# Five unrolled loops of the expert stage become hardware loops

## The reference, cut to what matters

```
idx = jnp.take_along_axis(cand_i, best_j, axis=-1)
gate = jax.nn.softmax(best_s, axis=-1)
act = jax.nn.gelu(jnp.einsum('thkd,td->thk', u_table[idx].astype(f32), xc.astype(f32)), approximate=False)
return jnp.einsum('thk,thkd->td', gate * act, v_table[idx].astype(f32)).astype(xc.dtype)
```

## Time and profile before

| | |
|---|---|
| median of 3 runs | 3418.4 us (3418.02 to 3423.0) |
| the profiled execution | 3418.02 us |
| its span | 3416.2 us |
| busy: PE, DVE, POOL, ACT | 2317.9, 2248.2, 1343.9, 1028.7 us |
| DMA moved | 1216.96 MB, 356 GB/s over the span |
| granted TensorE clock, mean | 0.826 |

### The profile page before, as it was taken

The page is one execution under the profiler, slowest core; times in us unless marked ns, Lnnn a source line. Parts: engine busy times, 40 slices in busy tenths (PEclk is TensorE's granted clock), DMA queues, the critical chain, the costliest instruction groups (busy, mean ns, idle before and its releaser), DMA issues.

```text
span 3416.2 us, 32073 instructions
## 1 busy us (share of the span) xinstructions
PE 2317.9 (68%) x9269; PEld 942.4 (28%) x9269; DVE 2248.2 (66%) x5256; ACT 1028.7 (30%) x3405; POOL 1343.9 (39%) x1241
## 2 busy tenths in 40 slices
PE   7997566575676567666765686568556856685576
PEld 4554443141133113211321142114112411151121
DVE  4433527879657955785578557856785677668754
ACT  2221213432332233223323332333233323333222
POOL 1131103334444444444444444444444444444532
PEclk9998788797788689868986888688768977897799
DMA  4222157999999999999999999999999999999998
GB/s 180 83 71 76 28 211 311 371 376 394 390 412 416 388 409 421 413 377 413 417 416 381 416 416 420 376 410 417 416 384 420 421 413 388 417 415 415 388 419 346
DMA packets 190072, 1216.96 MB, mean 356 GB/s; under 512 B 27112, under 2 KB 32664, under 8 KB 49176
## 3 DMA queue, kind: packets, MB, share of 16 engines
q0 software_dynamic: 157152, 1141.51, 82.4%
q1 hardware_dynamic: 30432, 71.87, 5.9%
q10 hardware_dynamic: 2312, 1.54, 0.2%
HBM read 1199.16 MB, written 15.55 MB: 356 GB/s over the span
## 4 chain that ended last, share of the span: by engine, by line
DMA 29%; DVE 24%; PE 21%; issue 6%; ACT 5%; POOL 2%; DVEq 0%; POOLq 0%; SPq 0%; PEldq 0%; ACTq 0%
DMA uv_ring<-in_uv_table,idx 28%; DVE uv_ring L1767 12%; PE ACC L1940 12%; PE TQ L1879 5%; POOL uv_ring L1419 2%; DVE S L1686 2%; DVE idx_f L1687 2%; DVE S L1685 2%; ACT dg L1541 2%; PE OP L1860 2%; PE TQ L1901 1%; ACT dot L1534 1%; ACT dot L1521 1%; PE ACC L1930 0%; DVE pos L1617 0%
## 5 line engine op out<-in xcount | busy, mean ns | idle before, releaser
L1940 PE MATMUL ACC<-uv_ring,dg 128*64 128x512 f32 x4352 | 1460.5, 782 | 957.0 <-ACT dg L1541 956.7
L1419 POOL DMA_INDIRECT uv_ring<-in_uv_table,idx x1088 | 1265.1, 1163 | 1707.6 <-PE ACC L1940 1402.8
L1767 DVE CUSTOM_DVE_ANT_0 uv_ring<-uv_ring,xn 128x1024 f32<-128x1024 f32 x1088 | 1322.6, 1226 | 712.8 <-DMA uv_ring<-in_uv_table,idx 668.9
L1940 PEld LDWEIGHTS ACC<-uv_ring,dg 128*64 128x64 f32 x4352 | 340.0, 165 | 1961.4 <-ACT dg L1541 1442.5
L1521 ACT ACTIVATE dot<-dot 128x2 f32<-128x2 f32 x544 | 110.6, 203 | 1798.5 <-DVE dot L1767 1798.2
L1541 ACT ACTIVATE dg<-stack,dot 128x64 f32<-128x64 f32 x1088 | 327.1, 340 | 17.8
L1534 ACT ACTIVATE dot<-gate,dot 128x1 f32<-128x1 f32 x1088 | 261.3, 287 | 18.9
L1879 PEld LDWEIGHTS TQ<-glu_and_queries,wq 128*128 128x128 f32 x2048 | 236.5, 193 | 62.8 <-issue 62.8
L1879 PE MATMUL TQ<-glu_and_queries,wq 128*128 128x128 f32 x2048 | 250.1, 280 | 0.0
L515 PE MATMUL PJ<-w_in,xT 128*128 128x512 f32 (+1 forms) x384 | 142.9, 532 | 3.2 <-DVE xT L401 3.2
L515 PEld LDWEIGHTS PJ<-w_in,xT 128*128 128x128 f32 x384 | 73.3, 193 | 72.3 <-issue 65.3
(11 more groups left out here) (338 smaller groups left out, 1696.3 us busy)
## 6 DMA issues: line engine op xcount, KB each, us to landing
uv_ring<-in_uv_table,idx POOLq DMA_INDIRECT x1088, 10.5
glu_and_queries<-in_w_glu SPq DMA_DIRECT2D x9, 1024.0 KB, 17.1
wq<-in_w_query SPq DMA_DIRECT2D x8, 1024.0 KB, 19.8
w_in<-in_w_in SPq DMA_DIRECT2D x8, 640.0 KB, 9.1
xt<-in_x SPq DMA_DIRECT2D x9, 512.0 KB, 4.6
xr<-scratch_x SPq DMA_DIRECT2D x9, 512.0 KB, 7.9
xc<-in_x_columns SPq DMA_DIRECT2D x8, 512.0 KB, 3.7
xk<-in_x SPq DMA_DIRECT2D x8, 512.0 KB, 3.4
```

The costliest lines, as they stand in the source:

```text
L1419: pool.indirect_dma_start(out=ring[:, s_ % RING, :], out_offset=None, in_=a["uv_table"], in_offset=bass.IndirectOffsetOnAxis(ap=idx[:, s_: ...
L1767: V.tensor_tensor_reduce(row, row, xn[:, g, :], 1.0, 0.0, ALU.mult, ALU.add, dot[:, s_:s_ + 1]).then_inc(dots, 1)
L1940: ins = nc.tensor.matmul(ACC[GT * g:GT * (g + 1), b, :], dg[:, n % DG, :], ring[:, n % RING, D + 512 * b:D + 512 * b + 512], start=False, ...
```

## The change

The loop over turns 1 to 6 on POOL, ACT, DVE and PE, and the loop over turns 0 to 6 on SP, become hardware loops (`Fori`): the body stands once in the program, a register holds t, and a compare-and-branch at its end jumps back. In the body every wait whose value depends on t takes it from a register, and so do SP's DRAM addresses. Turn 0, turn 7 and the samples stay written out.

DVE's own step count can no longer be a Python number, so `Steps` is replaced by `PerTile` there, which assumes 130 steps in a turn and adds t x 130 to a base.

```
+class PerTile:
+    def __init__(self, sem, per):
+        self.sem, self.n, self.base, self.per = sem, 0, 0, per
+    def chain(self, eng, t, ins, nop=False):
+        self.n += 1
+        ins.then_inc(self.sem, 1)
+        eng.wait_ge(self.sem, self.n if t is None else self.base + t * self.per + self.n)
+        if nop:
+            eng.nop(nofuse=True)
+    def loop_begins(self, t):
+        self.base, self.n = self.n - t * self.per, 0
+    def turn_ends(self):
+        assert self.n == self.per, (self.n, self.per)
+        self.n = 0
...
+        DVE_STEPS = 130
...
-        dch = c.steps("dve_steps_e")
+        dch = PerTile(c.sem("dve_steps_e"), DVE_STEPS)
...
-                for t in range(PT - 1):
+                with sp.Fori(0, PT - 1) as t:
...
-                for t in range(1, PT - 1):
+                with pool.Fori(1, PT - 1) as t:
...
-                for t in range(1, PT - 1):
+                with act.Fori(1, PT - 1) as t:
...
                 def dch_(ins, nop=False):
-                    dch.chain(dve, ins)
-                    if nop:
-                        dve.nop(nofuse=True)
+                    dch.chain(dve, turn_now[0], ins, nop)
...
-                for t in range(1, PT - 1):
+                dch.loop_begins(1)
+                with dve.Fori(1, PT - 1) as t:
                     retrieve("steady", t)
+                dch.turn_ends()
                 retrieve("eighth", PT - 1)
+                dch.turn_ends()
...
-                for t in range(1, PT - 1):
+                with pe.Fori(1, PT - 1) as t:
```

More of the change, by code:

```diff
@@ L1604, in _ @@
                 V = nc.vector
+                turn_now = [None]
                 def dch_(ins, nop=False):
-                    dch.chain(dve, ins)
-                    if nop:
-                        dve.nop(nofuse=True)
+                    dch.chain(dve, turn_now[0], ins, nop)
                 def best16(vals, where, src):
@@ L1787, in retrieve @@
                 def retrieve(turn, t):
+                    turn_now[0] = None if turn == "first" else t
                     for s_ in range(LEAD, slots_of(turn)):
```

## The result

| | median | range, runs |
|---|---|---|
| before, on the same chip | 3420.16 us | 3418.02 to 3423.0, 4 |
| after | 3442.47 us | 3440.05 to 3445.3, 4 |

A forecast was written before the change was run, and what follows sets the result against it. The kernel was taken as DMA-bound except in the matching stage, where DVE binds. 3418.0 + 0 (jumps) + 1.2 (ACT registers) + 0.3 (fetching) = 3419.5 us, no change; range 3414 to 3433 us.

The forecast's parts named there:

- What bounds the kernel: Over a turn of 337.3 us: DMA-bound, except 60 us of matching stage where DVE binds and a short dip between turns.
- The slack: Gather time from issue to landing above 5.3 us can be lost free: 5.8 us for DVE's slot 10, 4.1 for PE's slot 8.
- X: Stall of one engine at one jump back to the loop's head: taken as 3.9 us, with 0 and 8.8 kept.
- The stall of a jump: At each loop's end, the wait for program code: 3.9 us, from a small load of the same size, bounds 0 and 8.8.
- ACT, POOL, SP: nothing: At the turn's end, jumps on these three engines cost nothing; POOL's is hidden up to a stall of 7.8 us.
- The late slots of DVE are caught up: After a late slot behind the jump, DVE catches up, being busy only two thirds of the DMA-bound stretch.
- The sum with 8.8 us: At five turn ends, with the longest stall: PE 2.5 us too late, or 4.3 with DVE in full; 12 to 22 us.
- Rival 1: At turn ends the jumps lie bare, from a 6.3 us stall (PE) or 7.0 (DVE): 3426 to 3441 us; chance 0.22.
- The registers: Register operations at 0.1 us each: 1.2 us in all on ACT, in and behind the matching stage; nothing on DVE, POOL, PE.
- rival 2: In the matching stage, register operations bind DVE: 14 us slower at 0.1 us bared, 3434 us; chance 0.09.
- more to fetch, 0.3 us: Program fetching in each turn: about 510 more instructions, some 0.2 MB in all, entered in the sum as 0.3 us.
- What would show it: At ends of turns 1 to 5: DVE idle 2 to 4 us, slot 10's gather landing in some 8 us, DMA share unchanged.

The follow-up runs named there:

- e5: Kernel before, with 2000 satisfied waits more on SP, written out, in each of turns 0 to 6: 3457.8 us against 3425.94.
- e12: Kernel before, with 1000 satisfied waits more on SP, written out, in each of turns 0 to 6: 3442.82 us against 3420.99.
- e6: Kernel before, with four unused DVE operations behind norm_out of turns 1 to 5, next product 5.0 us late, no jump: 3439.64 us against 3425.94.
- e10: Kernel before, with two unused DVE operations behind norm_out of turns 1 to 5, next product 2.5 us late: 3426.79 us against 3420.99.
- e3: Changed kernel with the hardware loop on DVE only, the other engines' turns written out: 3438.86 us against 3421.92 before the change.
- e1: Changed kernel with its registers (SP has constants) but no jump back, each turn in a loop of one pass: 3429.63 us against 3421.92 before the change.
- e4: Changed kernel with the hardware loop on PE only, the other engines' turns written out: 3424.77 us against 3421.92 before the change.
- e8: Kernel before, with a hardware loop on PE only, with the prefetch hint for its jump: 3422.7 us against 3425.94.
- e9: Changed kernel with DVE alone written out again, all other loops kept: 3425.42 us against 3420.99 before the change.
- e7: Changed kernel with two turns in a body on POOL, ACT, DVE and PE, two jumps instead of five: 3438.05 us against 3425.94 before the change.

## Why the prediction was wrong

Its own steps, in its order:

- **What bounds the kernel.** Held. It is DMA-bound but for the matching stage: e5 and e12 lose time only outside it. (The DMA digits are 9 from the eighth slice on, not from the seventh, which reads 7; nothing hangs on it.)
- **The slack: the step that failed.** The prediction took what lies above 5.3 us between issue and landing as time that could be given away, and so 5.8 us for DVE and 4.1 for PE. 5.3 us is the least over all gathers, and it comes from a place where the DMA engines were not full: the gather was issued at 591 us, in turn 0. The window around it, the landings of gathers from 560 to 600 us, and those of the DMA-bound stretch of turn 1 (1250 to 1480 us), all of before:

```profile
586.00:596.00 10.00, 6.26 (x22) 1.81 (x24) 9.02 (x29) 4.88 (x14) 3.94 (x4) 0.81 0.55 211
```

```profile
DMA to landing us min/median/max: 5.3/7.7/10.2
```

```profile
DMA to landing us min/median/max: 7.3/11.4/17.3
```

  So a better bound, 7.3 us, stood in the trace of before. With it slot 8 has 2.1 us of slack and slot 10 3.8: for X = 3.9 still enough (1.7 and 2.7 late), for the stalls that came not (1.3 to 2.5 and 5.0 late). At the turn's end, with the gathers issued so late that few were on their way, a gather still needed 7.7 us at the least (gathers issued from 1250 to 1266 in the changed kernel; before, from 1243 to 1262, 9.4, 11.1 and 12.3):

```profile
DMA to landing us min/median/max: 7.7/8.2/10.1
```

  With 7.7 in place of 5.3 the slack of slot 8 is 9.4 - 7.7 = 1.7 us and of slot 10 3.4. e6 and e10 measured 2.3 and 1.3. A second fault is in the idea itself: a gather that lands 5.3 or 7.7 us after its issue did not wait, but the DMA engines are full only while several are on their way. Slots 8 and 9 are all that was issued between 1247 and 1261, and the rate was 291 to 329 GB/s against 381 to 428.
- **The stall of a jump.** X was taken as 3.9 us, with 0 and 8.8 as ends; it is 5.6 to 6.3 us on DVE (`norm_out` start to product), 4.7 to 7.1 us on ACT from the root to the table load, and by the prediction's rule X - 2.2 = 1.3 to 2.5 us some 3.5 to 4.7 us on PE. Inside the bounds, 2 us too small on DVE. This error alone would not have changed the answer: 6.3 us is below the 7.0 from which DVE's was to show. On the stall itself the trace agrees with the rule of the Trainium skill, "Runtime: NRT & Kernel Launch", section "Instruction fetch mechanics", that a taken branch to a target out of the window stops the engine until the block has come: DVE stood for 4.96 us with no data missing, and in e3 a packet of program starts inside the stall, where before has none.
- **ACT, POOL, SP: nothing.** Held. ACT's GELU behind its stall still waits 2.59 us for DVE, POOL's gathers wait for PE.
- **The late slots of DVE are caught up.** It did catch up, 2.3 us by slot 8. But that does not bring back what was not transferred: in e6 slot 3 of the next turn is still 2.6 us late.
- **The sum with 8.8 us**, 2.5 to 4.3 us at each of five jumps, 12 to 22 in all, holds the measured 15. That is luck: in this sum X was too large by some 3 us and DVE's slack by some 4, and the two errors came near to cancelling. Rival 1 named the right mechanism and the right place, PE and DVE too late for the gathers of slots 8 to 11, with a threshold that was too high by 4 us. Had the landings of before been read at this place (9.4 us at the least), slot 8 would have had no slack and slot 10 11.1 - 9.4 = 1.7 us. With X = 3.9 that makes 1.7 to 2.7 us a jump, by my estimate 8 to 14 us in all, and rival 1 the forecast.
- **The registers.** ACT's first diagonal stands 0.83 us behind the GELU instead of 0.75: +0.08, as forecast 0.1. In the matching stage nothing, so rival 2 is out. But the term "more to fetch, 0.3 us" is wrong by its kind: it divided bytes by the rate of all 16 engines. In e5 and e12 fetching cost 0.3 to 0.5 us a packet while the DMA engines were the limit, and registers with what they bring cost 7.7 us.
- **What would show it.** The gather into slot 10's place landed in 8.2 us (issued at 1261.38, taken at 1269.56), as foreseen, and I had taken that as the sign of a hidden stall. It was the sign of the opposite: a queue that is short. The DMA share fell from 1.01 to 0.91 to 0.99 behind each jump, which the prediction named as what would prove it wrong. Turn 1 took 341.3 us instead of 337.3.

The forecast failed by these two terms, the slack that it took from the wrong place and the fetching that it put at 0.3 us. The sum as the runs have it: DVE's lateness 13.7 (e6) and registers with fetching 7.7 (e1), 21.4 of 22.3 us.

## What to carry to other kernels

Slack in a DMA-bound stretch is not the longest wait minus the shortest landing of the whole run. Read the landings and the GB/s at the place in question, and ask how many transfers are on their way when the late one is issued; what DVE caught up later here did not bring back the transfers that did not run (where only PE was late, e4, a part came back). A hardware loop costs its jump where the engine that jumps closes the ring, so use the hint (here it took away 15 of 22 us), and count instruction packets as transfers: in a kernel that is DMA-bound, fewer of them were worth a little here (4 us for 33), many more were dear (31 us for 110).

## What was unexpected of the hardware

- A jump back over a body of a few hundred instructions stops DVE for 4.4 to 5.1 us beyond what lies under the operation before it, with one engine jumping (e3) as with five; with the hint, for nothing that can be seen.
- An 8 KB packet of program cost 0.34 us (e12) to 0.46 us (e5) of the whole when the DMA engines were full, and nothing in the matching stage. It was less for PE's packets (e8) and in e9.
- PE's loop with the hint is not fetched again (40 packets instead of 73), without it it is fetched more than unrolled code (85).
- PE's `begin` takes 3.77 us instead of 1.96 behind the jump of turn 1. It is not the jump itself: the same four matmuls take as long in before, at the ends of turns 3 and 5. The granted clock in that stretch is 0.50, the lower of its two levels, 1.2 GHz, after PE had waited 3.5 us for ACT's diagonals and worked for 3.7:

```profile
1913.35 3.75 PE L1930 MATMUL ACC<-xr,ident_d 128*128 128x512 f32 x4 [1.51 <-DVE S L1773]
```

  At the full clock they take 1.96 us, as in all five turns of e3, which loses 16.9 us nevertheless. Behind a stall of PE they were slow each time (2.8 to 3.8 us in all 17 of after, e4, e7 and e9). Whether the stall brings that about is not shown.
